# A third buffer for the last sample's keys, and one low weight half prepared later

## The reference

```python
def dsa_sample(q, k_new, v_new, qi, ki_new, wi, cache_k, cache_v, cache_kidx, page_table, topk):
    ki_past = cache_kidx[page_table].reshape(B, PAST_LEN, IDX_DIM)
    ki_all = jnp.concatenate([ki_past, ki_new.astype(ki_past.dtype)], axis=1)
    sc = indexer_scores(qi, wi, ki_all, q_pos[None], k_pos)
    _, idx = lax.top_k(sc, topk)                       # 256 of 2049 keys
    ...
    return sparse_attend(q, select(cache_k, k_new), select(cache_v, v_new), idx <= q_pos[None, :, None])
```

## Time and profile before

| what | value |
|---|---|
| median of 3 runs | 2438.32 us (2434.61 to 2441.36) |
| the profiled execution's own time | 2435.11 us |
| its span, first to last instruction | 2433.1 us |
| mean granted TensorE clock | 0.973 of full |
| PE busy | 2336.0 us, 96% of the span |
| DVE, ACT, POOL busy | 1764.4, 1102.3, 440.2 us |
| first stage of the attention ends on PE | at about 566.6 us |
| second stage of the attention | from there to about 769 us |

### The profile page before, as it was taken

How to read it: one execution, slowest core, us unless ns; L and a number is a source line. 1 busy time by engine, 2 the same in 40 slices (tenths; PEclk the granted TensorE clock), 3 DMA queues, 4 the chain that set the end, 5 groups by cost and what they waited for, 6 DMA issues and landing times.

```text
span 2433.1 us, 46305 instructions
## 1 busy us (share of the span) xinstructions
PE 2336.0 (96%) x18624; PEld 2200.7 (90%) x18624; DVE 1764.4 (73%) x2608; ACT 1102.3 (45%) x1958; POOL 440.2 (18%) x348
## 2 busy tenths in 40 slices
PE   7999999998699999999999999999998989999999
PEld 7999999876357999999999999999896779999999
DVE  7975985665543788488888488777667984795794
ACT  6543543255243455255455255333656542552452
POOL 0000058424202300000400000400573303000000
PEclk9999999997799999999999999999998989999999
DMA  3322334334432222222223232423361022123222
GB/s 125 105 96 95 105 98 144 98 113 126 155 139 88 69 99 98 85 101 90 102 88 105 86 105 90 146 87 121 132 244 67 1 83 90 70 100 108 87 95 98
DMA packets 53867, 251.45 MB, mean 103 GB/s; under 512 B 8576, under 2 KB 17920, under 8 KB 33856
## 3 DMA queue, kind: packets, MB, share of 16 engines
q1 hardware_dynamic: 47808, 220.79, 26.2%
q0 software_dynamic: 5888, 28.32, 3.4%
HBM read 233.58 MB, written 15.49 MB: 102 GB/s over the span
## 4 chain that ended last, share of the span: by engine, by line
PE 89%; DVE 6%; ACT 3%; issue 2%; DMA 0%; POOL 0%; DVEq 0%; ACTq 0%; POOLq 0%
PE acc L646 32%; PE acc L521 24%; PE acc L491 8%; PE acc L1431 4%; PE acc L2832 3%; PE acc L632 2%; PE acc L2901 1%; PE acc L1802 1%; PE acc L1525 1%; DVE wl L427 1%; PE acc L1838 1%; ACT wh L386 1%; PE acc L2950 1%; PE acc L1682 1%; PE acc L1826 1%
## 5 line engine op out<-in xcount | busy, mean ns | idle before, releaser
L646 PE MATMUL acc<-xa,wh 128*128 128x268 f32 (+1 forms) x2240 | 436.9, 286 | 5.2 <-DVE wl L1122 2.9
L646 PE MATMUL acc<-xe,wh 128*128 128x268 f32 (+1 forms) x2240 | 437.4, 286 | 0.3
L386 ACT ACTIVATE wh<-raw 128x2048 fp32r<-128x2048 f32 x113 | 216.4, 1915 | 406.2 <-PE acc L521 303.0
L646 PEld LDWEIGHTS acc<-xa,wh 128*128 128x128 f32 x2240 | 349.6, 189 | 7.3 <-issue 3.1
L646 PEld LDWEIGHTS acc<-xe,wh 128*128 128x128 f32 x2240 | 349.4, 189 | 1.1 <-DVE scr L1142 0.7
L646 PE MATMUL acc<-xe,wl 128*128 128x268 f32 (+1 forms) x1120 | 320.4, 286 | 0.0
L646 PE MATMUL acc<-xa,wl 128*128 128x268 f32 (+1 forms) x1120 | 320.2, 286 | 0.0
L521 PE MATMUL acc<-gh,wh 128*128 128x268 f32 (+1 forms) x1408 | 288.7, 286 | 10.3 <-DVE wl L427 8.9
L427 DVE TENSOR_TENSOR wl<-raw,wh 128x2048 fp32r<-128x2048 f32 x103 | 249.3, 2420 | 59.5 <-ACT wh L386 59.3
L521 PE MATMUL acc<-gl,wh 128*128 128x268 f32 (+1 forms) x1408 | 287.3, 285 | 0.0
L521 PE MATMUL acc<-gh,wl 128*128 128x268 f32 (+1 forms) x1408 | 287.1, 285 | 0.0
(11 more groups left out here) (561 smaller groups left out, 4893.4 us busy)
## 6 DMA issues: line engine op xcount, KB each, us to landing
raw<-in_w_ffn_in SPq DMA_DIRECT2D x88, 1024.0 KB, 4.9
raw<-in_w_ffn_out SPq DMA_DIRECT2D x32, 768.0 KB, 4.3
raw<-in_w_ssd_in SPq DMA_DIRECT2D x21, 1024.0 KB, 4.9
raw<-in_w_ffn_out SPq DMA_DIRECT2D x32, 640.0 KB, 3.8
raw<-in_w_attn_in SPq DMA_DIRECT2D x9, 1024.0 KB, 4.9
kic<-in_kpages SPq DMA_DIRECT2D x72, 128.0 KB
xT<-in_state_ssm SPq DMA_DIRECT2D x8, 1024.0 KB, 7.7
out_hs<-xT SPq DMA_DIRECT2D x8, 1024.0 KB, 3.9
```

The lines of the kernel that those rows point to most:

```text
L386: nc.scalar.activation(wh[:, slot], raw[:, slot], ACT.Copy).then_inc(wh_ready, 1)
L646: mm = nc.tensor.matmul(bank(n, number), w[:, slot, c:c + P], x_pair(f, low, i)[:, m0:m0 + hc], start=(number in (1, 2, 5) and i == 0 and ...
```

## The change

A tile `last_keys` of 128 x 4096 floats is put on the same memory as the two slots of `wl`. The keys of sample 7 are loaded there, all 16 pages by SP (`sp_last_keys`), once `chunk_done` says that PE has multiplied chunk 8 and so no longer reads `wl`. In SP's order this stands after the keys of sample 4 and ahead of those of samples 5 and 6. `raw 7` reads `last_keys` and waits for its own semaphore. Since `wl` now holds keys until `raw 7` is done, `rest(9)` leaves its place in the first stage: DVE does it in step 20 of the second stage, after a wait for `kv_used` at 10 (`raw 7` done) and ahead of `scale_out(1)`. SP's load of weight chunk 11 waits for `rest(9)` and moves with it. POOL's part is unchanged. The other samples' keys keep their buffers and their waits.

```diff
-    wh, wl = sb("wh", [P, 2, BLK * P], F32R), sb("wl", [P, 2, BLK * P], F32R)
+    wh = sb("wh", [P, 2, BLK * P], F32R)
+    low_ctx = ExitStack()
+    wl = sb("wl", [P, 2, BLK * P], F32R, low_ctx)
+    low_ctx.close()
+    last_keys = sb("last_keys", [P, 2 * BLK * P], F32)
...
+    REST_AT = 20
...
-    def sp_keys(sp, pair):
-        for q in range(2):
-            s = 2 * pair + q
-            sp.wait_ge(kv_used, s + 1)
-            for g in range(NPG if s == S - 1 else NPG // 2):
...
+    def sp_keys(sp, s):
+        sp.wait_ge(kv_used, s + 1)
+        for g in range(NPG // 2):
...
+    def sp_last_keys(sp):
+        sp.wait_ge(chunk_done, ATT_IN + 9 + CREDIT)
+        for g in range(NPG):
+            pg = page_of(sp, S - 1, g)
+            sp.dma_start(last_keys[:, g * 256:(g + 1) * 256],
+                         I["kpages"][ds(pg, 1)].rearrange("a p c -> p (a c)")).then_inc(last_keys_loaded, 16)
...
+        else:
+            pe.wait_ge(last_keys_loaded, 16 + 16 * NPG)
+        keys_of = (kv[:, s % 2] if s < S - 1 else last_keys[:]).rearrange("p (l j t) -> p t l j", l=P, t=2)
...
         out(7, 1)
-        rest(9)
         rounds(3, 10, 13)
         out(8, 0)
...
+            if n == REST_AT:
+                dve.wait_ge(kv_used, 2 + S)
+                rest(9)
             if n - 2 in SCALE_AT:
                 scale_out(SCALE_AT.index(n - 2))
...
-                for pair in range(1, S // 2):
-                    sp_keys(sp, pair)
+                for s in range(2, 5):
+                    sp_keys(sp, s)
+                sp_last_keys(sp)
+                for s in range(5, S - 1):
+                    sp_keys(sp, s)
                 sp_attention_outputs(sp)
```

More of the change, by code:

```diff
@@ L1247, in build @@
     kic_loaded = sem("kic_loaded")
-    sp_keys_loaded = x_loaded[0:2]
+    sp_keys_loaded, last_keys_loaded = x_loaded[0:2], gains_loaded
     pool_loaded = [sem("pool_loaded0"), sem("pool_loaded1")]
@@ L1343, in page_of @@
         return eng.value_load(pages[0:1, ds(s * NPG + g, 1)], min_val=0, max_val=POOL - 1)
-    def sp_keys(sp, pair):
-        for q in range(2):
-            s = 2 * pair + q
-            sp.wait_ge(kv_used, s + 1)
-            for g in range(NPG if s == S - 1 else NPG // 2):
-                pg = page_of(sp, s, g)
-                sp.dma_start(kv[:, q, g * 256:(g + 1) * 256],
-                             I["kpages"][ds(pg, 1)].rearrange("a p c -> p (a c)")).then_inc(sp_keys_loaded[q], 16)
+    def sp_keys(sp, s):
+        sp.wait_ge(kv_used, s + 1)
+        for g in range(NPG // 2):
+            pg = page_of(sp, s, g)
+            sp.dma_start(kv[:, s % 2, g * 256:(g + 1) * 256],
+                         I["kpages"][ds(pg, 1)].rearrange("a p c -> p (a c)")).then_inc(sp_keys_loaded[s % 2], 16)
+    def sp_last_keys(sp):
[4 more added lines that the diff above has]
+                         I["kpages"][ds(pg, 1)].rearrange("a p c -> p (a c)")).then_inc(last_keys_loaded, 16)
     def pool_keys(pool):
@@ L1676, in pe_raw_scores @@
             pe.wait_ge(sscore_copied, s + 1)
-        pe.wait_ge(sp_keys_loaded[s % 2], 16 + 16 * NPG // 2 * (s // 2 + (1 if s < S - 1 else 2)))
-        pe.wait_ge(pool_loaded[s % 2], 16 * NPG // 2 * (s // 2 + (1 if s < S - 1 else 0)))
-        keys_of = kv[:, s % 2].rearrange("p (l j t) -> p t l j", l=P, t=2)
+        if s < S - 1:
+            pe.wait_ge(sp_keys_loaded[s % 2], 16 + 16 * NPG // 2 * (s // 2 + 1))
+            pe.wait_ge(pool_loaded[s % 2], 16 * NPG // 2 * (s // 2 + 1))
+        else:
+            pe.wait_ge(last_keys_loaded, 16 + 16 * NPG)
+        keys_of = (kv[:, s % 2] if s < S - 1 else last_keys[:]).rearrange("p (l j t) -> p t l j", l=P, t=2)
         for t in range(2):
@@ L3563, in _ @@
                 sp_keys(sp, 0)
+                sp_keys(sp, 1)
                 sp.wait_ge(ki_ready, 1)
```

## The result

| | median of its runs | before, same chip | ratio, 95% interval |
|---|---|---|---|
| first measurement, 7 runs of each | 2421.24 us (2419.81 to 2428.69) | 2438.32 us | 0.9941, 0.9926 to 0.9955 |
| again, 12 runs | 2422.25 us | 2436.26 us | 0.9945, 0.9913 to 0.9978 |
| once more, on another chip, 12 runs | 2422.06 us | 2434.52 us | 0.9953, 0.9920 to 0.9986 |

The change makes the kernel faster, by 0.5 to 0.6%: 2438.32 x (1 - 0.9941) = 14.4 us in the first measurement, 13.4 and 11.5 us by the ratios of the other two. The plain differences of the medians are 17.1, 14.0 and 12.5 us.

A forecast was written before the change was run, and what follows sets the result against it. PE was taken to bound the kernel, busy 96% of the span, with a 12.14 us wait for sample 7's keys. 12.14 + 1.48 - 0.4 - 1.05 = 12.17 us off 2438.3 gave 2426 us, range 2418 to 2433 for 8 in 10.

The forecast's parts named there:

- The stall: PE's wait for keys ahead of the scores of sample 7 goes whole: 12.14 us gained.
- the clock behind it: Scores of sample 7 run at full clock, 1.93 us in place of 3.41: 1.48 us gained.
- the wait only moves: Rival: the stall moves to other scores or to the keys of samples 5 and 6; 2435 to 2440 us, chance 0.08.
- The mask: DVE's masking of samples 0 to 3 now waits for POOL's mask: 0.4 us off the gain.
- The first stage: The low half leaves DVE's first stage, but DVE waits for ACT's roots anyway: 0 gained, upper bound 2.29 us.
- Step 20: The low half delays DVE's scaling of an output group, so PE waits about 1.05 us: lost.
- the sum of 11.4 us: Gain in all if a POOL transfer met the low half in step 20 and lengthened it by 0.83 us.
- The sum: Whole kernel: 12.14 + 1.48 - 0.4 - 1.05 = 12.17 us gained, median 2426 us.
- the sum's base: Differences taken from the earlier kernel's median of 2438.32 us, 3.2 us above its profiled execution of 2435.11.
- More: Rival: two low-clock stretches behind the stall go too; 15 to 18.5 us gained, 2420 to 2423 us, chance 0.14.
- Less: Rival: step 20's hole lowers the clock (gain 9) or POOL's mask is slowed (8.5); 2429 to 2430 us, chance 0.15.
- Slower: Rival: step 20's hole keeps PE at the lower clock to the attention's end, costing 41 us; 2467 us, chance 0.05.

The follow-up runs named there:

- e2: Kernel before the change with only the low half moved to step 20, keys of sample 7 left as they were: 2438.12 us, ratio 0.9999.
- e3: Changed kernel with SP asking for the keys of sample 7 last, behind those of samples 5 and 6: 2437.35 us, ratio 1.0001 to the kernel before.
- e8: Same kernel as e3, keys of sample 7 asked for last, run again for a second profile: 2437.63 us, ratio 0.9985 to the kernel before.
- e4: Kernel before the change, no third buffer, with POOL loading pages 8 to 15 of sample 7: 2440.12 us, ratio 1.0013.
- e12: Changed kernel with POOL building the samples' mask before its first load of values: 2425.36 us, ratio 0.9961 to the kernel before.
- e1: Changed kernel run again without edit, for a second profile: 2422.25 us, ratio 0.9945 to the kernel before.
- e9: Changed kernel run a third time without edit, on another chip: 2422.06 us, ratio 0.9953 to the kernel before.
- e7: Changed kernel with the low half's subtraction made twice in step 20: 2429.58 us, ratio 0.9952 to the kernel before.
- e6: Changed kernel with the low half behind the scaling in step 20 and POOL's mask ahead of its first values: 2421.95 us, ratio 0.9934 to before.

## Why the prediction was right

**The stall (12.14 us) and the clock behind it (1.48).** Both as forecast: no wait, and 1.93 us. e2, e3 and e8 show that it is the place in SP's queue that pays: neither the low half's move nor the third buffer brings a measurable gain without it. SP's 16 requests ran from 569.96 to 587.00, forecast 570.2 to 587.6, and nothing behind them was late. So *the wait only moves* did not come about here; it did in e4.

**The mask (0.4).** 0.27 us of waiting, and 0.37 us to be had by e12. POOL was not slowed.

**The first stage (0).** e2 bears it out, with a ratio of 0.9999 and by its trace: 17.84 us for the stretch that took 17.68.

**Step 20 (1.05).** 1.04 us, in every execution that has the low half once in front. The low half took 2.28 us there and not 3.12. By the rule of the Trainium skill, SBUF — State Buffer, "Who interferes with whom", a DVE instruction with two inputs in SBUF contends with a GpSimd instruction that reads SBUF; in the first profile POOL runs none from 678.96 to 689.18, and the trace shows no lengthening, so the sum of 11.4 us by that rule did not apply.

**The sum.** 12.14 + 1.48 - 0.27 - 1.04 = 12.31 us from waits that are seen. e1's attention ends 14.15 us earlier. About 1.5 us more are the dip behind step 20, which e1 lacks and before has, and 0.41 us the work ahead of the scores (624.37 for 624.78); the sum is 14.2. Neither was forecast. The 0.41 is luck of this execution; the 1.5 is luck too if e1 went without the dip by chance, and a gain that the prediction did not see if the hole in step 20 keeps the dip away. Behind the attention nothing is won or lost: e1 took 14.09 us less in all than the profiled execution before. The first profile has the dip, starts the scores 1.93 us late and loses 48.90 - 46.56 = 2.34 us to the low clock between them and the first values: 12.31 - 1.93 - 2.34 = 8.0, measured 7.9.

**The time.** 2426 us was forecast and 2421 to 2422 measured, outside the 2424.5 to 2427.5 us that I counted as this case. The step that was off is the sum's base: I took the differences from the median of three runs, 2438.32 us, and the kernel before has had medians of 2436.26, 2436.48 and 2434.52 us since. From the profiled execution's own 2435.11 the same sum gives 2422.9; from the medians of e1's and e9's chips it gives 2424.1 and 2422.3, where 2422.25 and 2422.06 were measured. It does not explain the first measurement: there the seven runs before have a median of 2438.32 again, and 4.9 us are left over. The interval of that ratio, 11 to 18 us, covers the sum; more is not known of it.

**The rivals.** *More*: by the time alone it would have come true, for it named 2420 to 2423 us. The traces speak against it: the stretch of low clock at the masking stayed (PE waits 2.46 us for DVE at 637.26 and then takes 1.14 us for a pair's scores), as argued, and from the end of sample 7's scores to the first values e1 takes 44.63 us, before 44.25. *Less*: the hole of 3.36 us in e7 did cost clock, that of 1.04 us did not. By the Trainium skill, TensorE: Matmul & The Clock Gate, "HAM oscillation", repeated waits throttle the array again, and the work behind each starts cold; e7 agrees (0.69 behind its one hole), and the changed kernel does not show it behind its hole of 1.04 us (1.00). *Slower*: even behind the hole of 3.36 us the clock was back at 1.00 within 5 us.

**A sign that misled.** I had named a mask that ends after 633 us, and a clock below 1.00 between 662 and 695, as signs against the forecast. The first profile showed both (633.46, and 0.66 from 664 to 674), and e1 neither. Signs given as positions from the span's start were too narrow for a kernel whose executions drift by several us ahead of the change.

## What to carry to other kernels

When a transfer is late, look first at what it is queued behind and what its buffer waits for: a further buffer paid only together with an earlier place in the queue, into a time in which the queue was idle. Before moving work into a busy stage, add what it delays on the critical engine, and ask whether the hole is long enough to cost clock as well. For effects near 1 us, compare stretches between two events of the profile, and repeat the profile: totals of the same program differ by more.

## What the runs showed of the hardware

The same program ends several us earlier or later by where PE's low-clock stretches fall. Of the twelve executions of e9 eight had a mean granted clock of 0.975 or 0.976 and took 2419.6 to 2423.0 us, three had 0.970 and took 2428.7 to 2429.8, and one had 0.961 and took 2453.0. That spread is larger than either wait that the change brought in.

A PE that is busy by the profile is no guard against the lower level: in e6 it was busy 4.00 of 4.00 us from 700 to 704, with a granted clock of 0.57, and 9.88 of the 10 us before, at 1.00. In e1 it was busy all of the 19 us from 537 to 556, at 0.99 up to 551 and at 0.50 from there.

A page of 128 KB landed 2.0 us after its request in the median of e8, but the slowest of its sixteen took 8.1 us.
